# One inference step of a two-layer diffusion backbone: 48 modulation tiles move from the first attention into the first projection

## The chip, the cores and the metric

One core of a Trainium2 chip runs the whole step. The metric is the device time of one execution in microseconds, as the median of three runs, beside one execution that was profiled. TensorE multiplies matrices, VectorE and ScalarE work on tiles element by element, GpSimd issues the gathers and a few additions, SyncE issues the weight loads.

## The reference

Two trunk layers are computed for 512 latent tokens and 128 context tokens, width 1024, all in float32. Each layer does:

```
mod = SiLU(cond) @ w_mod[l] + b_mod[l]            # 6 x 1024 values; cond: c for latents, c_ctx for context
h   = RMSNorm(x) * (1 + scale1) + shift1
q, k, v = split(h @ w_in[l])                      # 1024 -> 2560, three head groups
o   = neighbourhood (A), differential (B) and grouped-query (C) attention
x   = x + gate1 * (o @ w_out[l])
h2  = RMSNorm(x) * (1 + scale2) + shift2
s   = top-16 of 128 x 128 product keys, 8 heads, of h2 @ wq
x   = x + gate2 * sum of 128 experts' v rows, weighted by gelu(u . h2) * softmax(s)
```

Context tokens read only context tokens; latents read their own keys and cached context keys. Every token has its own 128 experts, whose rows are gathered from memory (u and v, 8 KB a token and slot; 128 tokens make 1.05 MB a gather).

## The kernel before

One program holds an instruction list for each engine, and semaphores order them. The latent tokens go through the stages `norm`, `project` (20 blocks of 128 columns, `NWIN`), `attention` (80 score maps in 40 pairs: 12 pairs of group A, 16 of B, 12 of C), `out_projection` (8 blocks), `norm`, `queries` (16 blocks) and `experts` (4 x 128 slots), once a layer.

The context tokens' work is threaded through these as Python generators that each engine advances by hand. `ctx_front` is a list of steps (42 before its choice of experts): its own projection, attention, output projection and queries. The first layer's front runs in the first projection: `FRONT_P` says how many steps are advanced in each of four parts of a block, the parts standing behind the matmul pairs 1, 3, 5 and 7 (`PARTS`). Behind the 42 come 24 steps (`PICKS[0]`) in which only VectorE works: it picks the experts, one step in each part of blocks 7 to 12. `ctx_slots` then handles the context tokens' 128 expert slots: GpSimd gathers the rows (L1936), VectorE takes the dot product (L1744), ScalarE applies gelu, VectorE adds the scaled row two slots later (L1736). `ROW_CALLS` says how many slots ("calls") each engine does behind each block of the projection (P), pair of the attention (A), block of the output projection (O) and of the queries (Q). Which of nine row buffers a slot may use depends on the stages around it (`ctx_buffers`): five in the projection, six late in the attention and in the output projection, and at the seam to the queries only three.

The modulation is 48 tiles a layer (`mod_tile`: four matmuls of a 128 x 2 by 128 x 256 product over one 0.5 MB weight block), eight tiles a chunk, six chunks. ScalarE copies a finished chunk to a row (`mod_copy`, L1044), TensorE turns it (`mod_turn`, L647), VectorE adds the bias (`mod_add`, L1408). Chunks 0 and 1 of the first layer are made in the opening. `project_mods` puts chunks 2 to 5 behind blocks 0 to 3 of the first projection, eight tiles in a row. `pair_mods` puts the second layer's 48 tiles behind pairs 2 to 29 of the first attention, three, three and two in three pairs out of five; `pair_chunk` places the copy and the turn.

All weights come through one ring of four 0.5 MB buffers (`RING`). SyncE loads them in the order of `block_plan`, which repeats the order in which TensorE takes them, and waits before each until TensorE has released the buffer (L609).

In `project` TensorE waits at block i for the evacuation of block i - 2 by ScalarE, which itself has its slots of the block before ahead of it in its list. `post` adds a norm or rotation step behind blocks 4 to 15, and VectorE answers a block later. The attention starts for TensorE when all blocks are evacuated, for VectorE when it has done the projection's slots.

## Time and profile before

| | us |
|---|---|
| median of three runs | 4343.43 |
| lowest, highest | 4335.09, 4356.98 |
| the profiled execution, its own time | 4348.79 |
| its span, first to last instruction | 4346.8 |
| TensorE busy | 2888.6 (66%) |
| VectorE busy | 2806.7 (65%) |
| ScalarE busy | 1454.9 (33%) |
| GpSimd busy | 1292.9 (30%) |

The span is the time between the first and the last instruction of the profiled execution; its own time has 2.0 us more around it. Shares are means over stages that have different limits.
### The profile page before, as it was taken

The page shows a single profiled execution, that of the slowest core. Times are in us where ns is not written, and L with a number is a line of the kernel's source. Part 1 is how long each engine was busy: PE and PEld are TensorE (multiplying, and loading weights), DVE is VectorE, ACT ScalarE, POOL GpSimd, SP SyncE. Part 2 cuts the span into 40 slices and gives each one's busy share as a digit, 9 for nine tenths or more (in the row PEclk, how much of TensorE's full clock was granted, in tenths as well). Part 3 has the DMA queues.
Part 4 walks back from the last instruction along what each step waited for, and adds up shares of the span by engine and source line. Part 5 has one row for each costly group of instructions (what it writes and reads, how often), then busy time and mean ns, then how long its engine had stood idle before and what let it go on. Part 6 is the DMA issues. An engine that isn't in the chain of part 4 may idle for free.

```text
span 4346.8 us, 47495 instructions
## 1 busy us (share of the span) xinstructions
PE 2888.6 (66%) x16560; PEld 1298.9 (30%) x16560; DVE 2806.7 (65%) x5854; ACT 1454.9 (33%) x4676; POOL 1292.9 (30%) x1306
## 2 busy tenths in 40 slices
PE   7897688775666666655556978886555555555554
PEld 4456565331221122321111566543111111111111
DVE  2166887697646756665675789669764775775444
ACT  2113675332223322222223468533222222222222
POOL 1002222123333333333343222212333333333332
PEclk9898889987777778778777989997778778777777
DMA  7536997569999999999997678666999999999996
GB/s 280 204 133 259 349 378 254 206 254 404 403 407 404 403 408 407 409 412 420 418 414 310 251 253 289 224 227 249 413 420 418 412 414 418 413 416 415 416 416 283
DMA packets 229151, 1508.71 MB, mean 347 GB/s; under 512 B 25392, under 2 KB 27440, under 8 KB 63920
## 3 DMA queue, kind: packets, MB, share of 16 engines
q0 software_dynamic: 185504, 1353.53, 77.7%
q1 hardware_dynamic: 43408, 152.14, 9.5%
q8 instruction: 131, 2.15, 0.2%
q14 instruction: 108, 0.88, 0.1%
HBM read 1501.38 MB, written 4.19 MB: 346 GB/s over the span
## 4 chain that ended last, share of the span: by engine, by line
DMA 41%; PE 25%; DVE 20%; issue 6%; ACT 5%; POOL 2%; SPq 0%; DVEq 0%; ACTq 0%; POOLq 0%
DMA work<-expert_dram,work 38%; PE psum L848 10%; DVE work L1694 5%; PE psum L876 4%; DVE work L1736 4%; PE psum L695 3%; DVE work L1744 3%; PE psum L786 2%; POOL work L1954 2%; DMA ring<-w_mod_dram 2%; PE psum L699 2%; ACT work L1207 1%; PE psum L763 1%; DVE stat L1484 1%; ACT work L1198 1%
## 5 line engine op out<-in xcount | busy, mean ns | idle before, releaser
L848 PE MATMUL psum<-work 64*64 64x512 f32 x8192 | 1422.0, 825 | 1121.8 <-ACT work L1207 1087.9
L1694 DVE SCALAR_TENSOR_TENSOR work<-work,psum 128x1024 f32<-128x1024 f32 x1024 | 1247.3, 1220 | 1001.9 <-DMA work<-expert_dram,work 996.9
L1954 POOL DMA_INDIRECT work<-expert_dram,work x1024 | 983.1, 960 | 1722.9 <-PE psum L848 1586.8
L848 PEld LDWEIGHTS psum<-work 64*64 64x64 f32 x8192 | 329.6, 168 | 2157.7 <-ACT work L1207 1841.9
L1198 ACT ACTIVATE work<-work 128x2 f32<-128x2 f32 x512 | 104.1, 203 | 1926.6 <-DVE work L1694 1910.0
L1936 POOL DMA_INDIRECT work<-expert_dram,work x256 | 279.5, 1092 | 1207.6 <-DVE work L1736 888.3
L1744 DVE SCALAR_TENSOR_TENSOR work<-work 128x1024 f32<-128x1024 f32 x256 | 311.3, 1217 | 92.3 <-DMA work<-expert_dram,work 91.8
L1207 ACT ACTIVATE work<-const,work 128x128 f32<-128x128 f32 x1024 | 347.3, 386 | 0.0
L1736 DVE SCALAR_TENSOR_TENSOR work<-work 128x1024 f32<-128x1024 f32 x254 | 325.2, 1280 | 19.7 <-ACT work L1223 19.3
L800 PE MATMUL psum<-work,ring 128*128 128x512 f32 x512 | 234.9, 614 | 28.5 <-ACT work L1070 28.5
L1201 ACT ACTIVATE work<-work 128x1 f32<-128x1 f32 x1024 | 245.7, 287 | 16.8
L763 PE MATMUL psum<-work 128*128 128x128 f32 x1456 | 214.8, 308 | 39.4 <-ACT work L1132 24.0
L695 PE MATMUL psum<-work,ring 128*128 128x512 f32 x448 | 210.4, 619 | 12.2 <-ACT work L1070 12.1
L763 PEld LDWEIGHTS psum<-work 128*128 128x128 f32 x1456 | 196.3, 216 | 57.7 <-ACT work L1132 27.5
L876 PEld LDWEIGHTS psum<-work,ring 128*128 128x128 f32 x1216 | 153.1, 208 | 29.3 <-issue 26.9
L876 PE MATMUL psum<-work,ring 128*128 128x128 f32 x1216 | 157.6, 294 | 2.3 <-DMA ring<-w_in_dram 1.1
L747 PE MATMUL psum<-work 128*64 128x128 f32 x1136 | 90.5, 312 | 79.7 <-ACT work L1141 77.6
L800 PEld LDWEIGHTS psum<-work,ring 128*128 128x128 f32 x512 | 99.2, 199 | 144.4 <-issue 141.6
L1217 ACT ACTIVATE work<-work 128x1 f32<-128x1 f32 x256 | 50.3, 196 | 264.7 <-DVE work L1744 264.7
L1484 DVE TENSOR_REDUCE stat<-psum 128x1 f32<-128x640 f32 (+2 forms) x160 | 116.8, 759 | 25.9 <-PE psum L731 22.3
L1117 ACT ACTIVATE work<-psum,stat 128x640 f32<-128x640 f32 (+2 forms) x160 | 117.9, 738 | 26.2 <-DVE stat L1484 23.8
L695 PEld LDWEIGHTS psum<-work,ring 128*128 128x128 f32 x448 | 87.1, 199 | 120.6 <-issue 109.1
(197 smaller groups left out, 2864.9 us busy)
## 6 DMA issues: line engine op xcount, KB each, us to landing
ring<-w_mod_dram SPq DMA_DIRECT2D x96, 512.0 KB
ring<-w_in_dram SPq DMA_DIRECT2D x80, 512.0 KB
ring<-w_query_dram SPq DMA_DIRECT2D x64, 512.0 KB
work<-expert_dram,work POOLq DMA_INDIRECT x1280, 7.6
ring<-w_out_dram SPq DMA_DIRECT2D x32, 512.0 KB
work<-rpb_dram POOLq DMA_DIRECT2D x2, 2688.0 KB, 12.1
xT<-xT_dram SPq DMA_DIRECT2D x1, 2560.0 KB, 11.8
work<-tables_dram POOLq DMA_DIRECT2D x2, 1024.0 KB, 5.4
```

Of the source, the lines that this page charges most:

```text
L695: last = pe.matmul(out, w[:, k, :], h[:, k, :], start=(k == 0), stop=(k == KC - 1))
L763: last = pe.matmul(flat[:, at_:at_ + P], prob[:, n % NPROB, b * P:(b + 1) * P], shares_[:, n % 4, :], start=(n == first), stop=(n == end))
L800: last = pe.matmul(psum[:, s % 2, :], w[:, k, :], h[:, k, :], start=(k == 0), stop=(k == KC - 1))
L848: last = pe.matmul(out[to:to + HP, cols_], diag[tok, n % NDIAG, tok], rows[(SLOTS * t + s) % NBUF][tok, D + 512 * half:D + 512 * half + 51 ...
L876: last = pe.matmul(out, one, two, start=(k == 0), stop=(k == KC - 1))
L1201: act.activation(coef[:, s + k:s + k + 1], act_out[:, s + k:s + k + 1], ACT.Copy, scale=weight[:, t % 2, s + k:s + k + 1]).then_inc(coef_d ...
L1207: act.activation(diag[:, (n + k) % NDIAG, :], con("ident"), ACT.Copy, scale=coef[:, s + k:s + k + 1]).then_inc(diag_done, 1)
L1694: dve.scalar_tensor_tensor(u, u, 1.0, pair[0], ALU.mult, ALU.mult, accum_out=act_in[:, s:s + 1]).then_inc(dot_done, 1)
L1736: last = dve.scalar_tensor_tensor(csum, v, ccoef[:, s:s + 1], csum, ALU.mult, ALU.add)
L1744: dve.scalar_tensor_tensor(u, u, GELU_C, xrow, ALU.mult, ALU.mult, accum_out=cact_in[:, s:s + 1]).then_inc(ctx_dot, 1)
L1936: pool.indirect_dma_start(crows[b], None, a[f"expert{l}"], bass.IndirectOffsetOnAxis(cexpert[:, s:s + 1], 0)).then_inc(ctx_row_in[b], 16)
L1954: pool.indirect_dma_start(rows[m % NBUF], None, a[f"expert{l}"], bass.IndirectOffsetOnAxis(expert[:, t % 2, s:s + 1], 0)).then_inc(row_in[ ...
```

## The change

The second layer's 48 modulation tiles leave the first attention. They are taken in the first projection, blocks 7 to 18, one in each of the four parts of a block. The first layer's 32 tiles are no longer taken eight in a row but singly, between the steps of the front. `FRONT_SEQ` writes the order out: "f" a front step, "m" a tile of the first layer, "n" one of the second. In block 5 two front steps move from the first parts to the last. Chunks are copied a block after their last tile and turned two blocks after; the last of the second layer is turned at the head of the attention, which now waits for all twelve additions. The second layer's chunks use PSUM banks 6 and 7, and wait for the context work's last reads of them.

The context slots move too: the first projection takes 17 for 11 and starts them at block 13 instead of 17, the attention 68 for 76, the output projection 18 for 14, the norm behind it 2 (a new place), the queries 24 for 28. The second layer's counts stay. At its start GpSimd's first five gathers are issued ahead of the wait for the last residual and of the tables.

```diff
-FRONT_P = ([(1, 1, 1, 7), (1, 0, 0, 3), (1, 1, 1, 2), (1, 1, 1, 2), (1, 1, 1, 3), (1, 1, 1, 5), (1, 0, 0, 3)]
-           + [(1, 1, 1, 1)] * (PICKS[0] // 4) + [(0, 0, 0, 0)] * (NWIN - 7 - PICKS[0] // 4))
+FRONT_SEQ = [("fm", "fm", "fm", "mfmfmfmfmfmfmf"), ("fm", "", "", "mfmfmf"), ("fm", "fm", "fm", "mfmf"),
+             ("fm", "fm", "fm", "mfmf"), ("f", "fm", "f", "mfmfmf"), ("m", "m", "fm", "mfffffff"), ("f", "", "", "fff")]
+FRONT_SEQ += [("fn",) * 4] * (PICKS[0] // 4)
+FRONT_SEQ += [("n",) * 4] * (12 - PICKS[0] // 4)
+FRONT_SEQ += [("",) * 4] * (NWIN - len(FRONT_SEQ))
+FRONT_P = [[x.count("f") for x in parts] for parts in FRONT_SEQ]
+CHUNK_DONE = {chunk_place("m", c - 1): (0, c) for c in range(2, NCHUNK)}
+CHUNK_DONE.update({chunk_place("n", c + 1): (1, c) for c in range(NCHUNK)})
+CHUNK_COPY = {i + 1: x for i, x in CHUNK_DONE.items()}
+CHUNK_TURN = {i + 2: x for i, x in CHUNK_DONE.items()}
-ROW_CALLS = [dict(P=[0] * (NWIN - 3) + [3, 4, 4], A=shares(76, NPAIR), O=shares(14, KC), Q=shares(28, HC)),
-             dict(P=shares(28, NWIN), A=shares(60, NPAIR), O=shares(12, KC), Q=shares(29, HC))]
+ROW_CALLS = [dict(P=[0] + [0] * 13 + [2] * 4 + [3] * 3, A=shares(68, NPAIR), O=[3, 2, 2, 2, 2, 2, 2, 3] + [2],
+                  Q=shares(24, HC)),
+             dict(P=[0] + shares(28, NWIN), A=shares(60, NPAIR), O=shares(12, KC) + [0], Q=shares(29, HC))]
...
             def mod_tile(l, j):
-                if k == 0 and NCHUNK * l + c >= 2:
-                    pe.wait_ge(mod_read, NCHUNK * l + c)
+                if k == 0 and l == 0 and c >= 2:
+                    pe.wait_ge(mod_read, 3 if c == 5 else 2)
+                elif k == 0 and l:
+                    pe.wait_ge(*rd("ks", 0, 3))
+                    pe.wait_ge(*rd("ks", 0, 2))
+                    if c >= 2:
+                        pe.wait_ge(mod_read, NCHUNK * l + c - 1)
...
             def project(l, front):
-                            if l == 0 and 1 <= i < 5:
-                                mod_turn(0, 1 + i)
-                            for m, j in project_mods(l, i):
-                                mod_tile(m, j)
+                            if l == 0 and i in CHUNK_TURN:
+                                mod_turn(*CHUNK_TURN[i])
                         if l == 0 and k in PARTS:
-                            go(front, FRONT_P[i][PARTS.index(k)])
+                            for x in FRONT_SEQ[i][PARTS.index(k)]:
+                                if x == "f":
+                                    go(front, 1)
+                                else:
+                                    mod_tile(*next(mods[x]))
             def attention(l, front):
+                if l == 0:
+                    mod_turn(*CHUNK_TURN[NWIN])
+                    pe.wait_ge(mod_read, 2 * NCHUNK)
...
-                    for m, j in pair_mods(l, k):
-                        mod_tile(m, j)
-                    if pair_chunk(l, k, 4) is not None:
-                        mod_turn(l + 1, pair_chunk(l, k, 4))
...
             def norm(ni, slots):                       # VectorE
+                calls = norm_calls(ni)
+                go(slots, (calls + 1) // 2)
                 dve.wait_ge(sum_step, KC * (ni + 1))
...
         def _(pool):
                 if l:
+                    pool.wait_ge(row_used, SLOTS * LT * l)
+                    calls += ROW_CALLS[l]["P"][0]
+                    ctx_gather(l, calls)
                     pool.wait_ge(y_added, LT * l)
...
-                if l:
-                    ctx_gather(l, 0)
```

## Rows read from the trace of the kernel before

**Rows 1.** Windows: microseconds, busy time (instructions) by engine, granted clock, DMA share, GB/s.

```profile
core 0: us, PE busy (x) PEld busy (x) DVE busy (x) ACT busy (x) POOL busy (x), PEclk, DMA share, GB/s
45.00:203.00 158.00, 131.91 (x822) 79.64 (x822) 33.30 (x49) 31.06 (x63) 11.82 (x6) 0.81 0.62 215
203.00:270.00 67.00, 63.28 (x453) 53.27 (x453) 24.29 (x85) 8.86 (x15) 0.00 (x0) 1.00 0.67 233
270.00:335.00 65.00, 57.36 (x127) 24.80 (x126) 62.15 (x162) 9.18 (x15) 0.00 (x0) 0.95 0.18 58
335.00:399.40 64.40, 47.19 (x406) 45.10 (x404) 32.94 (x50) 15.68 (x50) 13.82 (x13) 0.91 0.68 251
399.40:704.60 305.20, 228.85 (x1976) 171.03 (x1976) 257.54 (x434) 217.50 (x653) 77.91 (x77) 0.87 0.90 345
798.40:971.00 172.60, 134.33 (x395) 67.54 (x395) 143.26 (x379) 55.94 (x155) 36.56 (x32) 0.89 0.64 241
971.00:2270.00 1299.00, 787.93 (x4796) 276.07 (x4796) 824.59 (x1887) 360.04 (x1280) 471.98 (x483) 0.77 1.00 408
2525.00:2765.10 240.10, 189.95 (x1540) 153.85 (x1541) 218.23 (x378) 190.40 (x566) 61.80 (x60) 0.91 0.75 264
```

**Rows 2.** Waits of TensorE from 45 to 203: total us, times, longest.

```profile
PE psum L636 <- DMA ring<-w_mod_dram: 18.4, 21, 3.9
```

**Rows 3.** Windows of the modulation tiles' line alone (L636), eight records a tile.

```profile
45.00:203.00 158.00, 26.95 (x256) 4.14 (x256) 0.81 0.62 215
399.40:704.60 305.20, 27.32 (x384) 7.56 (x384) 0.87 0.90 345
```

**Rows 4.** Timeline of TensorE: start, length, what, records, idle before and its releaser.

```profile
56.59 1.48 PE L636 MATMUL psum<-ring,cT 128*2 128x256 f32 x24
...
123.81 9.82 PE L876 MATMUL psum<-ring,work 128*128 128x128 f32 x64 [1.66 <-DMA ring<-w_in_dram]
...
228.28 14.45 PE L876 MATMUL psum<-work,ring 128*128 128x128 f32 x128
```

**Rows 5.** Timeline of VectorE: end of the picks, first and last context slot's dot.

```profile
335.62 0.23 DVE L1897 TENSOR_SCALAR work<-work 128x128 f32<-128x128 f32 x1
...
353.78 1.22 DVE L1744 SCALAR_TENSOR_TENSOR work<-work 128x1024 f32<-128x1024 f32 x1
...
396.02 1.22 DVE L1744 SCALAR_TENSOR_TENSOR work<-work 128x1024 f32<-128x1024 f32 x1 [2.91 <-DMA work<-expert_dram,work]
```

**Rows 6.** Waits of TensorE from 203 to 399.4.

```profile
PE psum L683 <- DVE work L1460: 3.4, 1, 3.4
```

**Rows 7.** Timeline of TensorE: a value block (14), the attention's first scores.

```profile
335.63 7.31 PE L699 MATMUL psum<-ring,work 128*128 128x128 f32 x64
...
382.14 0.70 PE L729 MATMUL psum<-work 64*128 64x256 f32 x4 [1.75 <-ACT work L1091]
```

**Rows 8.** DMA issues on the page: engine, count, median us from issue to landing.

```profile
work<-expert_dram,work POOLq DMA_INDIRECT x1280, 7.6
```

**Rows 9.** Groups of VectorE's instructions: first attention, then second attention.

```profile
L1736 DVE SCALAR_TENSOR_TENSOR work<-work 128x1024 f32<-128x1024 f32 x75 | 95.9, 1279 | 1.7 <-ACT work L1223 1.7
L1744 DVE SCALAR_TENSOR_TENSOR work<-work 128x1024 f32<-128x1024 f32 x75 | 91.3, 1218 | 21.0 <-DMA work<-expert_dram,work 20.6
...
L1744 DVE SCALAR_TENSOR_TENSOR work<-work 128x1024 f32<-128x1024 f32 x59 | 71.7, 1215 | 4.2 <-DMA work<-expert_dram,work 4.2
```

**Rows 10.** Timeline of VectorE: dots of context slots 100, 102 and 105.

```profile
788.90 1.22 DVE L1744 SCALAR_TENSOR_TENSOR work<-work 128x1024 f32<-128x1024 f32 x1 [5.62 <-DMA work<-expert_dram,work]
...
809.99 1.22 DVE L1744 SCALAR_TENSOR_TENSOR work<-work 128x1024 f32<-128x1024 f32 x1 [5.98 <-DMA work<-expert_dram,work]
...
836.58 1.22 DVE L1744 SCALAR_TENSOR_TENSOR work<-work 128x1024 f32<-128x1024 f32 x1 [6.42 <-DMA work<-expert_dram,work]
```

**Rows 11.** The norm products of the second layer's start (L1440): shortest, median, longest ns.

```profile
L1440 DVE TENSOR_TENSOR work<-xT,work x8: 679/2223/2226, 2363.9 to 2375.9; 128x512 f32<-128x512 f32 x8
```

More of the change, by code:

```diff
@@ L115 @@
 A_MAPS = 2 * A_PAIRS
-MOD_PAIR = 2
-MOD_CYCLE = 5
 GELU_C = math.sqrt(2.0 / math.pi)
@@ L263, in front_blocks, with mod_order @@
     return [[next(blocks) for _ in range(n)] for n in FRONT_BLOCKS] + [[]] * PICKS[l]
+def mod_order():
+    return {"m": iter([(0, j) for j in range(16, NMOD)]), "n": iter([(1, j) for j in range(NMOD)])}
 def block_plan():
@@ L269, in block_plan @@
     for l in range(L):
-        front = iter(front_blocks(l))
+        front, mods = iter(front_blocks(l)), mod_order()
         for i in range(NWIN):
             plan.append(("win", l, i))
-            for p in range(len(PARTS)):
-                if p == len(PARTS) - 1:
-                    plan += [("mod", m, j) for m, j in project_mods(l, i)]
-                if l == 0:
-                    for _ in range(FRONT_P[i][p]):
-                        plan += next(front)
-        for k in range(NPAIR + 2):
-            plan += [("mod", m, j) for m, j in pair_mods(l, k)]
+            for seq in FRONT_SEQ[i] if l == 0 else ():
+                for x in seq:
+                    plan += next(front) if x == "f" else [("mod", *next(mods[x]))]
         plan += [("wout", l, i) for i in range(KC)]
@@ L675, in post @@
                     pe.wait_ge(post_fin, POSTS * l + p - 1)
+                if l == 0 and p == 1:
+                    pe.wait_ge(mod_read, 4)
                 if what == "norm":
@@ L1052, in square, with norm @@
                 act.activation(sq[:, c % 2, :], xT[:, c, 0:NLAT], ACT.Square).then_inc(sq_ready, 1)
-            def norm(ni):
+            def norm(ni, slots):
                 if ni == 0:
@@ L1358, in _ @@
                 slots = ctx_slots(l)
-                norm(2 * l)
+                norm(2 * l, slots)
                 project(l, front, slots)
@@ L1362, in _ @@
                 out_projection(l, slots)
-                norm(2 * l + 1)
+                norm(2 * l + 1, slots)
                 queries(l, slots)
@@ L1366, in _ @@
                 experts(l, front)
-            norm(2 * L)
+            norm(2 * L, None)
         @block.vector
@@ L1414, in mod_add, with root, norm @@
                         [P, KC, 2]), ALU.add, ALU.mult))
-            def root(l, i, ps, n):
+            def root(l, i, ps, n, slots=None, calls=0):
                 dve.tensor_scalar(var, ps, 1.0 / n, EPS, ALU.mult, ALU.add).then_inc(var_ready, 1)
+                go(slots, calls)
                 dve.wait_ge(sd_ready, roots(l, i))
                 link(dve.reciprocal(rs, var))
-            def norm(ni):
+            def norm(ni, slots):
                 l, half = ni // 2, ni % 2
+                calls = norm_calls(ni)
+                go(slots, (calls + 1) // 2)
                 dve.wait_ge(sum_step, KC * (ni + 1))
@@ L1431, in norm @@
                 else:
-                    root(l, 5 if half else 0, psum[:, 2, :], D)
+                    root(l, 5 if half else 0, psum[:, 2, :], D, slots, calls // 2)
                 if ni == 2 * L:
@@ L1902, in _ @@
                 slots = ctx_slots(l)
-                norm(2 * l)
+                norm(2 * l, slots)
                 project(l, front, slots)
@@ L1906, in _ @@
                 out_projection(l, slots)
-                norm(2 * l + 1)
+                norm(2 * l + 1, slots)
                 queries(l, slots)
@@ L1910, in _ @@
                 experts(l, front)
-            norm(2 * L)
+            norm(2 * L, None)
         @block.gpsimd
@@ L1990, in _ @@
                     ctx_gather(l, calls)
+                calls += ROW_CALLS[l]["O"][KC]
+                ctx_gather(l, calls)
                 pool.wait_ge(ctx_added, SLOTS * l + last_slot(l, (3, 4, 5)) + 1)
```

48 lines of the change are left out of this document (25 added, 23 removed).

## The prediction

> **What bounds the kernel now.** I read the busy times by stage first, then who waited for whom on TensorE and VectorE, then the timelines at the seams between stages. The stage table [rows 1] shows four kinds of stretch. In the experts (971 to 2270) the DMA share is 1.00 at 408 GB/s: nothing here touches it. The first projection (45 to 399.4) is TensorE's: 131.91 of 158 us busy up to 203, 63.28 of 67 to 270; then VectorE is the one that is full, 62.15 of 65. The first attention (399.4 to 704.6, first to last softmax exponential) shows VectorE busy for 257.5 of 305.2 us and the DMA engines 0.90 busy. The second layer's attention, the same 40 pairs without modulation tiles and with 60 context-expert calls for 76, takes 240.1 with VectorE 218.2 and DMA 0.75 [rows 1]. So the DMA load is what is crowded in the first attention, and hardly used (0.18) at 270 to 335, where tiles are to go.
>
> **Term 1, blocks 0 to 6 (45 to 203): first layer's 32 tiles singly.** Now they come eight at a time behind blocks 0 to 3, and a ring of four buffers cannot feed eight in a row: TensorE waits 18.4 us for them in 21 waits [rows 2], and its 32 tiles are 26.95 us busy [rows 3], with 3.2 us more for a projection weight that stands behind a batch in the DMA queue (I take 3 from the timeline; the first such wait is 1.66, [rows 4]). Together 48 us. A tile that lies in the ring costs 1.48/3 = 0.49 us [rows 4]; 32 of them 16 us. Fed singly, each lies beside a front step of two blocks or a pair of matmuls. Supply: one tile is 0.524 MB, at 408 GB/s 1.28 us; a modulation tile and two context blocks are 3.9 us of transfer beside 0.49 + 2 x 1.8 = 4.1 us of TensorE. It just fits, with little slack in block 0, where 4.5 MB of tables and bias (11 us) land as well. Gain 48 - 16 = 32. The clock: 64 context matmul records at 123.81, behind a batch, take 9.82 us, and 128 at 228.28 take 14.45 [rows 4], that is 2.6 us more for the first; the granted clock is 0.81 here and 1.00 from 203 to 270 [rows 1]. Four such restarts are some 9 us; I take 5. Against it: a batch hid the ScalarE and VectorE latency of the context attention, whose scores, softmax and turns now follow each other closer; I charge 4. Term 1: -34 (bounds -20, if block 0 and the chain take half back, to -43).
>
> **Term 2, blocks 7 to 19 (270 to the first exponential at 399.4).** Added: 48 tiles at 0.49 = 23.5 us of TensorE, and the turns, copies and additions of six chunks, which move along and are small; 1 us of VectorE's is counted in Term 3, and TensorE's in the 3 us below. In blocks 7 to 13 VectorE is the bound: its picks run without a gap up to 335.6 [rows 5], TensorE is idle 7.6 of 65 us [rows 1] and waits for it, as 3.4 us in one place [rows 6]. 28 tiles are 13.7 us, 7.6 of it in that idle time; block 13 ends some 3 to 4 us later. If that cover is gone the tiles cost 13.7. Blocks 14 to 19 are bare TensorE work now, 7.31 us each [rows 7]; 20 tiles add 9.8, so the projection ends at 382.1 + 13 = 395 (in old times). But its end did not matter: TensorE was ready at 382.1 [rows 7] and the first exponential ran at 399.4, since VectorE and ScalarE still had slots 0 to 10 to finish, the last at 396.0 [rows 5]. With 17 slots instead of 11, and from block 13 instead of 17, the first dot moves from 353.8 to about 345 (335.6 and a gather's issue and landing, 7.6, [rows 8]), then five buffers, freed two slots late, let three slots pass in the 7.6 us of a landing and the 2.5 us of VectorE's two passes, 3.5 us a slot: slot 16 at about 395 to 398. Both chains end together; the addition of the last chunk and TensorE's new wait for it, ahead of the first scores, put 2 us behind (what is queued behind that wait is the whole attention).
> The resource that gets tight is DMA: from 335.6 on, 22 ring tiles (11.5 MB) and 17 rows of 1.05 MB (17.8 MB) are 29.4 MB, at 408 to 420 GB/s 70 to 72 us, so 406 to 408, and 2 us behind. Now: 399.4. Term 2: +10, with 6 more slots done by then. Bounds: -3 (rows need not all have landed, slots overlap) to +25.
> A rule against the change: the Trainium skill, DMA: Bandwidth & Descriptors, section Specifications, gives about 358 GB/s as the HBM limit of one core; by it the 29.4 MB would be an estimated 82 us and Term 2 +21. This trace moved 408 GB/s over 1299 us [rows 1], so the row is taken.
> New waits on TensorE: the first tile of a chunk waits for the read of its bank (6 or 7) by ScalarE or VectorE two blocks back, already done, so I charge nothing; the rest of its block is queued behind it, and a wait of a microsecond in each of six would be inside the bounds. SP issues the 48 loads in the new order, each as its buffer falls free, and so ahead of TensorE by up to four; in the attention it has then only four output blocks in the ring. GpSimd's gathers stand in their own queue.
>
> **Term 3, the first attention.** It loses 48 tiles (27.32 us of TensorE, [rows 3]; 25.2 MB, 61 us of DMA) and 8 of its calls. A call is a dot and an addition: 1.218 + 1.279 = 2.5 us of VectorE [rows 9]. VectorE's work becomes 257.5 - 8 x 2.5 - 1 = 236.5. What is left is its idle time: 47.7 us now, 20.6 of it for rows that had not landed [rows 9], against 21.9 and 4.2 in the second layer's attention [rows 1, 9]. With rows alone in the DMA queues (71 MB in 260 us, 274 GB/s) I take the second layer's idle time scaled to 68 calls, 24. 236.5 + 24 = 261 for 305.2: -44. Bounds: idle time stays 47.7, -21; it falls to 10, -58.
>
> **Term 4, output projection, norm, queries.** The output projection gets 18 calls for 14, and the norm behind it 2; the queries 24 for 28. With 2.4 us a call and 0.75 for the residual of a block against some 7.7 us of TensorE, as in the first projection (7.31 and more), two calls hide and three just do. In block 7 and the norm they don't: at the seam only three row buffers suit both stages, so each slot waits for a whole gather, 5.6 and 6.4 us at 788.9 and 836.6 [rows 10]. By the kernel's buffer rule 8 slots are so bound now, two of them ahead of the norm; after it 6, all in the queries, and two of distance four in the norm. I count about +4 ahead of the queries (the norm's first call waits some 6 us for its row, the second hides ScalarE's root) and +2 in their first four steps; behind these VectorE is full (143.3 of 172.6 for the stage, the rest mostly those waits, [rows 1]) and has 4 calls less, -10. Term 4: -4 (bounds +8, -12).
>
> **Term 5, start of the second layer.** Five gathers are issued some 8 us earlier, ahead of the tables. They landed before their use already. They may let the bias land sooner, and GpSimd's mask additions with it, beside which VectorE's eight norm products take up to 2226 ns for 679 [rows 11]. Here the Trainium skill (SBUF — State Buffer, Who interferes with whom) says that such a two-input operation and GpSimd's block each other. An earlier start could save some 4 us; but tables and bias wait for the same event as before. -1 (0 to -4).
>
> **Sum.** -34 + 10 - 44 - 4 - 1 = -73. The profiled execution took 4348.8 (span 4346.8): 4276. The median of the three runs is 4343.4, 5.4 lower, so 4271 as a time.
>
> **Rivals.** (a) The rows' latency, not the DMA load, binds the first attention: only 8 calls and a few us go, -20 for -44: 4295. For it: five or six buffers stay, and a gather takes 7.6 us to land [rows 8]. Against: 20.6 us of row waits at DMA 0.90, 4.2 at 0.75, with the same buffers. (b) Ring loads and rows halve the queues in blocks 13 to 19: 17.8 MB at 205 GB/s are 87 us, 335.6 + 87 = 423 for 408: 4286. Against: the ring has 11.5 MB to send in that time, less than half. (The Trainium skill, the same DMA page, section Queues, rings and completion order, says that each DMA engine takes its queues in turn; by that an equal split while both are full.) (c) Blocks 0 to 6 are bound by supply; half of Term 1 stays: 4288. For it: the slack of 0.2 us in 4.1 above. (d) Slower: the slots of blocks 13 to 19 stand on ScalarE ahead of the next block's evacuation, so a row that comes late holds TensorE, which then frees no ring buffer. If each of 17 slots costs a bare round trip as at the queries' seam, 8.9 us (836.6 less 810.0 is three of them, [rows 10]), they end at 345 + 151 = 496, 97 late and not 10: 4358. It makes the whole change a loss from 83 us late on, 8.1 us a slot for the 3.5 I take; five buffers for three speak against it. (e) The edit does what it says: the tiles cannot stay in the attention, so no case for that.
>
> **How the numbers follow.** Forecast 0.62 (own range 4250 to 4292); (a) 0.13; (b) 0.08; (c) 0.10; (d) 0.03, and 0.04 for a cost that I don't see; these two lie around no change. The range 4244 to 4305 holds the forecast and (a) to (c). A change under 0.5% (22 us) can't be told from none here: faster 0.93, same 0.04, slower 0.03 (the tails of (d) and of the unseen).
>
> **What would show it.** Waits of TensorE for modulation tiles up to 203 fall from 18.4 us to under 6. The first exponential comes at about 375 (399.4 - 34 + 10). The attention takes 250 to 272, DMA share near 0.7, VectorE's waits for rows under 8 us. Granted clock from 45 to 203 above 0.9. The picks end near 302. If the first exponential is later than 390, or the attention longer than 280, I am wrong in Term 2 or 3; a wait for a row in each of slots 5 to 16 would be (b) or (d).

## The result, and the profile after

| | before | after |
|---|---|---|
| median of six runs each, us | 4337.43 | 4380.80 |
| lowest, highest, us | 4328.82, 4356.98 | 4376.05, 4384.29 |
| the profiled execution's span, us | 4346.8 | 4380.4 |

The ratio is 1.0091, 95% interval 1.0076 to 1.0106: slower by 0.9%, where 4271 was forecast. The first view of the new kernel is the busy time by stretch (columns as in [rows 1]). The first two rows are the same times as there; the third begins near the start of block 7, the fourth at the end of the picks, the fifth at the first softmax exponential. The sixth is the queries, up to the first expert's dot product at 1011.3; before, that dot product came at 967.5, so the row of [rows 1] that ends at 971.0 is 3.5 us too long for this comparison.

```profile
45.00:203.00 158.00, 131.91 (x847) 85.44 (x847) 35.67 (x51) 29.45 (x59) 12.46 (x7) 0.90 0.61 221
203.00:270.00 67.00, 57.41 (x382) 45.51 (x383) 23.13 (x81) 9.16 (x17) 0.00 (x0) 0.90 0.59 199
270.00:365.40 95.40, 79.09 (x357) 29.13 (x355) 63.46 (x168) 12.33 (x24) 0.00 (x0) 0.89 0.44 162
365.40:493.50 128.10, 92.79 (x652) 65.84 (x654) 47.50 (x70) 28.50 (x91) 23.58 (x19) 0.79 0.76 292
493.50:753.40 259.90, 193.83 (x1550) 156.54 (x1546) 236.90 (x401) 199.45 (x597) 70.80 (x68) 0.91 0.77 275
848.50:1011.30 162.80, 131.53 (x392) 66.48 (x392) 130.33 (x359) 52.11 (x142) 30.37 (x28) 0.90 0.65 239
```

The attention, in the fifth row, has become 45.3 us shorter (305.2 in [rows 1], 259.9 here), as forecast. All of that and more is lost ahead of it: the first exponential comes at 493.5, not at 399.4. By stage, after less before: block 7 starts 4.4 later (274.4 for 270.0); from there to the first exponential +89.7 (219.1 for 129.4); the attention -45.3; output projection and norm +1.3; queries up to the first expert -6.3; the first layer's experts -5.9; the second layer's projection -3.6. That is +34.3 of the 33.6 between the spans.

What TensorE waited for, from 45 to 270, to 365.4, and to 493.5 (total us, times, longest; the modulation tiles' line is now L651):

```profile
PE psum L651 <- DMA ring<-w_mod_dram: 20.2, 8, 3.9
PE psum L1017 <- DVE work L1804: 6.5, 1, 6.5
...
PE psum L651 <- DMA ring<-w_mod_dram: 12.1, 5, 2.8
PE psum L713 <- DMA ring<-w_in_dram: 2.7, 5, 0.8
...
PE psum L651 <- DMA ring<-w_mod_dram: 26.2, 7, 6.5
PE psum L717 <- DMA ring<-w_in_dram: 5.2, 6, 3.2
PE psum L752 <- DVE modT L1426: 2.5, 1, 2.5
```

That is twenty waits for a tile with 58.5 us, for all 80 tiles. Before, the 32 tiles of the first layer waited 18.4 us [rows 2], and the 48 others in the attention another 15.8 (waits of TensorE, 399.4 to 704.6):

```profile
PE psum L636 <- DMA ring<-w_mod_dram: 15.8, 6, 3.7
```

So 34.2 us in 27 waits have become 58.5 in twenty. The timeline of TensorE over one block shows where they stand (start, length, what, records, idle before and its releaser):

```profile
303.09 1.03 PE L651 MATMUL psum<-ring,cT 128*2 128x256 f32 x8 [2.82 <-DMA ring<-w_mod_dram]
304.49 2.90 PE L713 MATMUL psum<-work,ring 128*128 128x512 f32 x4 [0.36 <-DMA ring<-w_in_dram]
307.32 0.61 PE L651 MATMUL psum<-ring,cT 128*2 128x256 f32 x8
307.86 1.98 PE L713 MATMUL psum<-work,ring 128*128 128x512 f32 x4
...
312.23 0.61 PE L651 MATMUL psum<-ring,cT 128*2 128x256 f32 x8
312.78 1.98 PE L713 MATMUL psum<-work,ring 128*128 128x512 f32 x4
314.60 1.02 PE L700 MATMUL psum<-work,const 128*128 128x512 f32 x2
318.17 0.61 PE L651 MATMUL psum<-ring,cT 128*2 128x256 f32 x8 [2.55 <-DMA ring<-w_mod_dram]
```

Only the last tile of a block waits, then the next block's weight behind it, and then one pair of matmuls takes 2.90 us where the others take 1.98. SyncE's own queue says why; this is its timeline over the same time:

```profile
284.58 15.19 SPq L619 DMA_DIRECT2D ring<-w_mod_dram  x4
299.82 0.43 SPq L619 DMA_DIRECT2D ring<-w_in_dram  x1
300.30 14.82 SPq L619 DMA_DIRECT2D ring<-w_mod_dram  x4
```

The ring has four buffers, and entry n lies in buffer n mod 4. A block's weight keeps its buffer until the block's last pair. The fourth entry behind that weight is the block's fourth tile (the order is weight, tile, tile, tile, tile), and it needs this very buffer. So its load is issued only when the block is over, at about 299.8, and TensorE stands until it has landed. That is a matter of the place in the ring, not of bandwidth: the DMA share in this stretch is 0.44.

The groups of TensorE's instructions from block 7 to the first exponential, before (270 to 399.4) and after (270 to 493.5), price it:

```profile
L695 PE MATMUL psum<-work,ring 128*128 128x512 f32 x112 | 50.5, 605 | 0.0
L699 PE MATMUL psum<-ring,work 128*128 128x128 f32 x384 | 43.4, 275 | 0.0
```
```profile
L713 PE MATMUL psum<-work,ring 128*128 128x512 f32 x112 | 63.1, 691 | 3.5 <-DMA ring<-w_in_dram 3.5
L717 PE MATMUL psum<-ring,work 128*128 128x128 f32 x384 | 59.0, 319 | 5.2 <-DMA ring<-w_in_dram 5.2
L651 PE MATMUL psum<-ring,cT 128*2 128x256 f32 x384 | 35.4, 447 | 38.3 <-DMA ring<-w_mod_dram 38.3
```

48 tiles are 35.4 us of TensorE (0.74 each, for the 0.49 of the forecast), 38.3 of waits for them, 8.7 of waits for weights, and the same 496 projection matmul records take 28.2 us more: 110.6 us where 23.5 were charged. 94.1 us of it show at the first exponential (493.5 for 399.4); the rest went into time in which TensorE had been idle (129.4 less 57.36 and 47.19, 24.9 us, [rows 1]).

In blocks 13 to 19 the context slots suffer from it. VectorE, from the end of the picks, waits for TensorE's turns, whose additions stand ahead of its slots (view: waits of VectorE, 365.4 to 493.5; below it, its timeline):

```profile
DVE modT L1426 <- PE psum L662: 51.0, 3, 19.0
DVE work L1765 <- DMA work<-expert_dram,work: 20.5, 5, 6.8
```
```profile
365.42 0.23 DVE L1918 TENSOR_SCALAR work<-work 128x128 f32<-128x128 f32 x1
...
374.42 1.22 DVE L1765 SCALAR_TENSOR_TENSOR work<-work 128x1024 f32<-128x1024 f32 x1 [6.84 <-DMA work<-expert_dram,work]
...
400.27 0.17 DVE L1426 TENSOR_TENSOR modT<-psum,cols 128x16 f32<-128x16 f32 x1 [18.96 <-PE psum L662]
```

The first attention's waits for rows, against 20.6 in [rows 9]:

```profile
L1765 DVE SCALAR_TENSOR_TENSOR work<-work 128x1024 f32<-128x1024 f32 x67 | 81.6, 1217 | 8.6 <-DMA work<-expert_dram,work 8.3
```

### The profile page after: what moved, and what is told of

Its sections match the earlier page's. It is cut to its first block, busy times and chain, and to the rows that moved or that the text cites. A ratio compares the mean times of both kernels' runs of the same rounds, so it can differ in the third digit from the quotient of the medians.

```text
span 4380.4 us, 47502 instructions
## 1 busy us (share of the span) xinstructions
PE 2922.1 (67%) x16560; PEld 1309.6 (30%) x16560; DVE 2803.7 (64%) x5854; ACT 1453.1 (33%) x4676; POOL 1305.4 (30%) x1306
## 4 chain that ended last, share of the span: by engine, by line
DMA 40%; PE 28%; DVE 19%; issue 6%; ACT 5%; POOL 2%; SPq 0%; DVEq 0%; ACTq 0%; POOLq 0%
DMA work<-expert_dram,work 37%; PE psum L867 10%; DVE work L1715 5%; PE psum L713 4%; DVE work L1757 4%; PE psum L895 4%; DVE work L1765 3%; PE psum L805 3%; PE psum L717 2%; POOL work L1975 2%; DMA ring<-w_in_dram 2%; ACT work L1225 1%; DVE stat L1507 1%; PE psum L786 1%; PE psum L651 1%
## 5 line engine op out<-in xcount | busy, mean ns | idle before, releaser
L819 PE MATMUL psum<-work,ring 128*128 128x512 f32 x512 | 232.1, 608 | 30.3 <-ACT work L1089 30.3
L1219 ACT ACTIVATE work<-work 128x1 f32<-128x1 f32 x1024 | 245.7, 287 | 16.8
L713 PE MATMUL psum<-work,ring 128*128 128x512 f32 x448 | 223.0, 641 | 15.0 <-ACT work L1089 9.7
L786 PE MATMUL psum<-work 128*128 128x128 f32 x1456 | 214.1, 307 | 25.5 <-ACT work L1146 10.8
## 6 DMA issues: line engine op xcount, KB each, us to landing
work<-rpb_dram POOLq DMA_DIRECT2D x2, 2688.0 KB, 15.8
xT<-xT_dram SPq DMA_DIRECT2D x1, 2560.0 KB, 11.7
```

What stands on the lines that cost most here:

```text
L713: last = pe.matmul(out, w[:, k, :], h[:, k, :], start=(k == 0), stop=(k == KC - 1))
L786: last = pe.matmul(flat[:, at_:at_ + P], prob[:, n % NPROB, b * P:(b + 1) * P], shares_[:, n % 4, :], start=(n == first), stop=(n == end))
L819: last = pe.matmul(psum[:, s % 2, :], w[:, k, :], h[:, k, :], start=(k == 0), stop=(k == KC - 1))
L1219: act.activation(coef[:, s + k:s + k + 1], act_out[:, s + k:s + k + 1], ACT.Copy, scale=weight[:, t % 2, s + k:s + k + 1]).then_inc(coef_d ...
```

## The experiments

Each was compared with the kernel before on the same chip. The three groups (e1 to e4, e5 to e7, e8 to e11) ran on different chips; across groups the ratios to before are what can be compared. The table cuts every profile at three events: the start of block 7, the first exponential, the last exponential. All but the first two rows are explained below.

| kernel | block 7 starts | to first exponential | attention | ratio to before [95%] |
|---|---|---|---|---|
| before | 270.0 | 129.4 | 305.2 | |
| after | 274.4 | 219.1 | 259.9 | 1.0091 [1.0076, 1.0106] |
| e1_m_only | 269.2 | 130.3 | 307.4 | 1.0002 [0.9987, 1.0017] |
| e2_n_only | 267.6 | 222.1 | 273.4 | 1.0135 [1.0116, 1.0153] |
| e3_rows_only | 266.5 | 132.9 | 299.8 | 0.9974 [0.9962, 0.9985] |
| e4_two_n | 269.1 | 144.1 | 287.3 | 0.9988 [0.9975, 1.0001] |
| e5_own_all | 244.6 | 187.8 | 260.3 | 0.9958 [0.9944, 0.9971] |
| e6_own_old_slots | 244.9 | 180.5 | 275.2 | 0.9993 [0.9979, 1.0006] |
| e7_two_n_new_slots | 266.7 | 141.7 | 272.0 | 0.9935 [0.9916, 0.9954] |
| e8_own_late_add | 246.0 | 192.3 | 263.5 | 0.9991 [0.9977, 1.0005] |
| e9_own_m_two_n | 242.4 | 143.9 | 274.0 | 0.9912 [0.9883, 0.9940] |
| e10_own_first_half | 245.7 | 150.0 | 281.0 | 0.9927 [0.9905, 0.9949] |
| e11_own_m2_two_n | 242.7 | 142.7 | 274.2 | 0.9879 [0.9851, 0.9906] |

**The parts one by one (e1 to e4).** e1: the first layer's tiles singly, the rest as before.

```diff
-FRONT_SEQ += [("fn",) * 4] * (PICKS[0] // 4)
-FRONT_SEQ += [("n",) * 4] * (12 - PICKS[0] // 4)
+FRONT_SEQ += [('f', 'f', 'f', 'f')] * (PICKS[0] // 4)
+FRONT_SEQ += [('', '', '', '')] * (12 - PICKS[0] // 4)
```

The second layer's 48 tiles are back in pairs 2 to 29, and `ROW_CALLS` as before.

> One part alone: the first layer's 32 tiles go singly as in the change (the front's order too), the second layer's 48 stay in the attention's pairs, slots as before. Theory R (ring order): tile or block number four behind a projection weight needs that weight's ring buffer, so its load starts only when the weight is released and TensorE waits a whole landing, 2.5 to 3 us, there. Then the stretch up to block 4's end gains some 17 us as in the changed kernel (202 to 185), blocks 5 and 6 give it back (tiles and the shifted front steps, a wait of 6 us for the context norm), and the total is within 10 us of before. Theory D (DMA bandwidth and slots in blocks 13 to 19 alone are at fault): this part keeps what I had forecast, 25 to 34 us faster than before.

4344.87 for 4343.77: no change. The waits up to block 7:

```profile
PE psum L674 <- DMA ring<-w_mod_dram: 18.4, 8, 3.4
PE psum L1045 <- DVE work L1836: 6.3, 1, 6.3
```

Spread out, the tiles wait as long in total as in batches, 18.4 us, in 8 waits for 21. Block 5 starts 12.4 us earlier than before (202.4 for 214.8), and then takes 44.6 us for 32.3: two front steps were moved to its end, and there TensorE waits 6.3 us for VectorE's norm of the context tokens (L1836), for 2.1 before.

e2: the second layer's tiles alone, with the first layer's in batches and the slots where they were.

```diff
-FRONT_SEQ = [("fm", "fm", "fm", "mfmfmfmfmfmfmf"), ("fm", "", "", "mfmfmf"), ("fm", "fm", "fm", "mfmf"),
+FRONT_SEQ = [("f", "f", "f", "mmmmmmmmfffffff"), ("f", "", "", "mmmmmmmmfff"), ("f", "f", "f", "mmmmmmmmff"),
...
```

> One part alone: the 48 second-layer tiles move into blocks 7 to 18, one per part, the first layer's stay eight in a row, slots as before (11 in the projection, from block 17). Theory R: every block from 7 to 18 takes 15 to 16 us for 7.8, with a wait of 2 to 3 us for the fourth tile and 0.3 to 0.8 for the next weight, so the first exponential comes 75 to 90 us later than 399.4, the attention is some 30 us shorter, and the total is 40 to 60 us slower than before. Theory D: blocks 7 to 12 take 10 us, blocks 13 to 18 suffer only from rows; with 11 late slots the first exponential is at most 20 us late and the total is 10 to 25 us faster.

4401.41, and the first exponential 90 us late: this part alone brings the whole loss. Its waits for tiles from 270 to 395:

```profile
PE psum L650 <- DMA ring<-w_mod_dram: 24.5, 9, 6.7
```

e3: the slots alone, with the second layer's earlier gathers (shown against the kernel before).

```diff
-ROW_CALLS = [dict(P=[0] * (NWIN - 3) + [3, 4, 4], A=shares(76, NPAIR), O=shares(14, KC), Q=shares(28, HC)),
+ROW_CALLS = [dict(P=[0] + [0] * 13 + [2] * 4 + [3] * 3, A=shares(68, NPAIR), O=[3, 2, 2, 2, 2, 2, 2, 3] + [2],
+                  Q=shares(24, HC)),
```

> One part alone: the new slot counts and places (17 in the projection from block 13, 68, 18 + 2, 24) and the second layer's earlier gathers, modulation tiles as before. Theory R: the slots are no cost; the first exponential within 5 us of 399.4, the attention 10 to 20 us shorter for 8 calls less, total 10 to 25 us faster. Theory S (slots that stand on ScalarE and VectorE ahead of the projection's evacuations hold TensorE back): first exponential 20 us or more later, total slower than before.

4334.81, 0.26% faster. The 17 slots are done when 11 were (first exponential at 399.4 in both), and the attention is only 5.4 us shorter (10 to 20 were expected), with the tiles still in it: VectorE has 18.6 us less to do (238.9 for 257.5) but is idle for 60.9 us there instead of 47.7.

e4: as e2, but two tiles a block, so that 24 of the 48 stay in the attention.

```diff
-FRONT_SEQ += [("fn",) * 4] * (PICKS[0] // 4)
-FRONT_SEQ += [("n",) * 4] * (12 - PICKS[0] // 4)
+FRONT_SEQ += [('f', 'fn', 'f', 'fn')] * (PICKS[0] // 4)
+FRONT_SEQ += [('', 'n', '', 'n')] * (12 - PICKS[0] // 4)
```

> A changed size: two second-layer tiles a block (parts 3 and 7) in blocks 7 to 18 instead of four, that is 24 tiles; the other 24 stay in the attention, in pairs 2 to 16. First layer's eight in a row, slots as before. Theory R: a ring of four then holds a weight, two tiles and the next weight, nothing stands fourth, so waits for modulation tiles in blocks 7 to 18 are under 5 us in all; first exponential at most 15 us later than 399.4, attention 10 to 20 us shorter, total 0 to 15 us faster than before. Theory T (each single tile costs TensorE several us whatever the ring does, by its weight loads or the granted clock): half of e2's loss in the projection, 35 to 45 us.

4337.63, with an interval that still touches no change. There are three entries a block now: the third behind a weight is the next block's weight, and the fourth, which needs this weight's buffer, is the next block's first tile and not one that this block needs. From 270 to 400 one wait for a tile is left, and SyncE's queue is no longer held for a block (its timeline below it):

```profile
PE psum L674 <- DMA ring<-w_mod_dram: 2.7, 1, 2.7
```
```profile
286.10 0.80 SPq L640 DMA_DIRECT2D ring<-w_mod_dram  x2
287.53 0.33 SPq L640 DMA_DIRECT2D ring<-w_in_dram  x1
```

The same order with half the tiles costs 14.7 us up to the first exponential, for 92.7 in e2. A cost of several us for every single tile, whatever the ring does, is excluded by this. But e4 halves the number of tiles along with their places in the ring, so it does not show alone how much of e2's loss is the ring; e5 does. A deeper ring for the same order (six buffers, by the same count, for five entries a block) was not tried.

**The tiles in buffers of their own (e5, e6, e8).** Two 0.5 MB buffers in idle work space, with their own semaphores, take the 32 and the 48 tiles out of the ring. The order of e5 is that of the changed kernel. One of the context slots' five row buffers had to be given up in the projection.

```diff
+def own(key):
+    return key[0] == "mod" and (key[1] == 1 or key[2] >= 16)
...
+                if own(key):
+                    n = OWN[key]
+                    if n >= 2:
+                        sp.wait_ge(own_freed[n % 2], n // 2)
...
+                    sp.dma_start(own_home(key), weights[what][l, i]).then_inc(own_landed[n % 2], 16)
-    sets = {"P": (0, 1, 2, 7, 8), "A": (0, 1, 2, 3, 8), "B": (0, 1, 2, 3, 4, 5), "O": (0, 1, 2, 3, 4, 5),
+    sets = {"P": (0, 1, 2, 7, 8) if l else (0, 1, 2, 8), "A": (0, 1, 2, 3, 8), "B": (0, 1, 2, 3, 4, 5), "O": (0, 1, 2, 3, 4, 5),
```

> The suspected cause alone taken away: the changed kernel, order of TensorE's work and slots as they are, but the 80 modulation tiles of both layers that are taken in the projection get two buffers of their own (space idle at that time; the first layer's context slots give up one of five row buffers in the projection for it). The ring of four then holds only projection and context weights. Theory R: waits for modulation tiles fall from 20 + 33 us to under 8, the picks end at 300 to 315 for 365, first exponential at 370 to 395 for 493, and the total is 4265 to 4300, 40 us or more faster than before: my forecast's terms hold once the ring is out of the way. Theory T (single tiles cost more than their records; clock, weight loads) or a share of VectorE waiting for TensorE's turns: picks still after 340, total within 15 us of before or slower.

4326.70: 1.3% faster than the changed kernel by the two ratios, but far from the forecast; the picks end at 319 and the first exponential comes at 432.4, so neither theory fits whole. Its waits, up to 270 and then to 432:

```profile
PE psum L1048 <- DVE work L1835: 9.0, 1, 9.0
PE psum L682 <- DMA work<-w_mod_dram: 4.0, 3, 1.8
...
PE psum L682 <- DMA work<-w_mod_dram: 12.7, 5, 4.3
PE psum L783 <- DVE modT L1457: 10.7, 1, 10.7
```

Block 5 starts at 179.1, 35.7 us ahead of before, which is Term 1's gain; block 5 itself then gives back 11 (43.3 us for 32.3). From block 7 to block 13 a block takes 11.6 us, for 15.5 in the changed kernel and 9.3 before. But from block 13 to the first exponential it is 118.4 us, for 73.7 before. VectorE waits there for rows and for the turns, while the DMA share is 0.85:

```profile
DVE work L1796 <- DMA work<-expert_dram,work: 35.0, 10, 5.8
DVE modT L1457 <- PE psum L693: 28.6, 3, 11.8
```

From block 7 to the first exponential the ring out of the way is worth 31.3 us (187.8 for 219.1), 23.6 of them ahead of block 13. That is a third of the 89.7; 58.4 are left. The two new buffers are a ring too, of two entries, and SyncE now waits for them and hardly for the ring of four (waits of SyncE's queue, 270 to 432.4):

```profile
SPq L642 <- PE psum L682: 110.9, 38, 7.6
SPq L647 <- PE psum L748: 13.2, 2, 10.0
```

e6 is e5 with the slots at their old counts and places (`ROW_CALLS` of before): are the early slots at fault?

> As e5, but with the slots before (11 in the projection from block 17, 76, 14, 28; gathers in their old place). It tells what the slots add once nothing stalls. Theory R with my Terms: the first exponential is as early or some us earlier than e5's, the attention 15 to 25 us longer, total 5 to 20 us slower than e5. If the earlier slots hold the projection (VectorE waits for turns of chunks ahead of its slots in every second block), e6 is as fast as e5 or faster.

4336.76, slower than e5. From block 13 to the first exponential it still takes 113.8 us, with 11 slots for 17, and so the slots are not what makes it long. Here TensorE is through block 19 at 398.6 and then waits for the last chunk's addition, which stands on VectorE behind the slots: the wait that I had priced at 2 us.

```profile
PE psum L782 <- DVE modT L1456: 17.1, 1, 17.1
```

Block 13 alone takes 19.0 us. SyncE's queue (first) and TensorE (second) show how long it is from issue to use once gathers are under way:

```profile
318.88 0.43 SPq L646 DMA_DIRECT2D ring<-w_in_dram  x1
320.97 17.62 SPq L641 DMA_DIRECT2D work<-w_mod_dram  x4
```
```profile
326.71 0.61 PE L681 MATMUL psum<-work,cT 128*2 128x256 f32 x8 [3.04 <-DMA work<-w_mod_dram]
330.56 3.76 PE L747 MATMUL psum<-ring,work 128*128 128x128 f32 x16 [3.23 <-DMA ring<-w_in_dram]
```

The weight that was issued at 318.88 could first be used at 330.56, 11.7 us later, and the four tiles behind it held SyncE's one list for 17.6 us: they have buffers of their own, but stand in the same list of loads, and the weight had waited in that list behind the tiles of block 13.

e8 is e5 with the additions behind the slots of a block on VectorE, not ahead.

```diff
-                    if l == 0 and i in CHUNK_TURN:
+                    if l == 0 and i in CHUNK_TURN and CHUNK_TURN[i][0] == 0:
                         mod_add(*CHUNK_TURN[i])
...
                     go(slots, ROW_CALLS[l]["P"][i + 1])
+                    if l == 0 and i in CHUNK_TURN and CHUNK_TURN[i][0]:
+                        mod_add(*CHUNK_TURN[i])
```

> e5 (own buffers for all 80 tiles) with one order changed on VectorE: the addition of a second-layer chunk, which waits for TensorE's turn at a block's end, stands behind the block's context slots and not ahead of them. Theory V (in e5 the slots from block 13 on are held by these waits, 12 + 10 + 7 us in three blocks): from the picks' end (319) to the first exponential 85 to 100 us for 113, total 10 to 25 us faster than e5's 4327. Theory L (row landings and the ring's loads share the DMA engines, so a slot takes 5 to 6 us whatever stands ahead of it): under 8 us faster than e5.

4332.15, not faster than e5. VectorE waits 23.2 us for turns, 28.4 for rows and 10.9 for ScalarE, together as long as e5's 63.6: the order on VectorE was not what held the stretch.

**Fewer tiles where they are dear (e7, e9, e10, e11).** e7 is e4 with the new `ROW_CALLS`, all in the ring.

> e4's placing (two second-layer tiles a block, 24 in all, the rest in the attention) with e3's slots. If the two gains add: 6 + 9 us, some 15 us faster than before, 4325 to 4332. If they collide (17 slots from block 13 on behind VectorE's wait for turns), it is no faster than e3 alone, 4335.

4311.57. That is 29 us, nearly twice the sum of e3 and e4 (9 and 6): with 24 tiles gone from the attention, its 8 fewer calls count, 272.0 us for 287.3 in e4, where with all 48 in it they brought 5.4 (e3).

e9 is e7 with two changes to the first layer's 32 tiles: they go singly, in the order of the changed kernel, and have e5's separate buffers, at a time when the row buffers are still idle, so that all five can stay. The second layer's 24 stay in the ring. e1 has shown that the order alone brings nothing. The edit of `own` against e5:

```diff
 def own(key):
-    return key[0] == "mod" and (key[1] == 1 or key[2] >= 16)
+    return key[0] == "mod" and key[1] == 0 and key[2] >= 16
```

> Own buffers for the first layer's 32 single tiles only; second layer's as in e7 (two a block in the common ring, 24 of 48, the rest in the attention), slots as the change has them. Theory R: blocks 0 to 4 as in e5, block 5 starts at about 179 for 210, block 5 keeps its wait of 9 us for the context norm, so blocks 7 on come 20 us earlier than in e7 and stay so: total 4290 to 4297, e7's 4311 less 15 to 20. Rival: the stretch behind the picks absorbs it (rows bind), under 8 us faster than e7.

4296.99, 0.2% under e7 by the ratios, whose intervals overlap. Block 7 starts at 242.4 for 266.7 in e7, 24.3 us earlier; 20.1 of it are left at the last exponential (660.3 for 680.4). The two profiled spans are only 6.5 us apart (4297.9 for 4304.4), since e9's profile is longer in the experts, whose code is the same: 1376.0 for 1367.8 from the first to the last dot product of the first layer's.

e10 moves the same 24 tiles, but four a block into blocks 7 to 12, with buffers of their own and none from block 13 on.

```diff
-FRONT_SEQ += [('f', 'fn', 'f', 'fn')] * (PICKS[0] // 4)
-FRONT_SEQ += [('', 'n', '', 'n')] * (12 - PICKS[0] // 4)
+FRONT_SEQ += [('fn', 'fn', 'fn', 'fn')] * (PICKS[0] // 4)
+FRONT_SEQ += [('', '', '', '')] * (12 - PICKS[0] // 4)
```

> e5 cut to the tiles that lie under VectorE's picks: four second-layer tiles a block in blocks 7 to 12 (24), own buffers, the other 24 in the attention; slots as the change has them. Term 2's claim is that these are hidden: picks end as in e5, 317 to 321, and blocks 14 to 19 run at 7.2 to 8 us each; first exponential at 385 to 400 for e5's 432, attention 10 to 15 us longer than e5's 260, total 4300 to 4312. If instead TensorE's added work in blocks 7 to 12 is what delays the picks, they end no earlier than e7's less 20, 312, and the total is above 4315.

4306.43. With no tiles behind block 13, 17 slots and four row buffers, block 13 to the first exponential takes 84.2 us, for 118.4 in e5. So 34.2 us of what e5 lost there was the doing of the tiles behind block 13. The attention, with 24 tiles in it, is 281.0 us, 20.7 longer than e5's where 10 to 15 were expected, and longer than e9's 274.0; why was not looked into.

e11 is e9 with the wait in block 5 taken away: the two front steps go back, and the tiles behind them move to earlier blocks.

```diff
-FRONT_SEQ = [("fm", "fm", "fm", "mfmfmfmfmfmfmf"), ("fm", "", "", "mfmfmf"), ("fm", "fm", "fm", "mfmf"),
-             ("fm", "fm", "fm", "mfmf"), ("f", "fm", "f", "mfmfmf"), ("m", "m", "fm", "mfffffff"), ("f", "", "", "fff")]
+FRONT_SEQ = [("fm", "fm", "fm", "mfmfmfmfmfmfmf"), ("fm", "", "m", "mfmfmfm"), ("fmm", "fmm", "fm", "mfmfm"),
+             ("fm", "fm", "fm", "mfmf"), ("fm", "fm", "fm", "fff"), ("f", "f", "f", "fffff"), ("f", "", "", "fff")]
```

> e9 with the first layer's tiles put earlier (10, 6, 8, 5, 3 in blocks 0 to 4, none in block 5) and the front's steps of block 5 as before the change (1, 1, 1, 5), since chunk 4, which the context's second norm needs, is then turned a block earlier. Theory N (the shifted steps of block 5 leave VectorE's norm bare behind the block, 9 us): block 5 takes 30 to 34 us for 43, TensorE's wait for the norm is under 3 us, total 5 to 12 us faster than e9, the fastest version. Rival: block 5 gains but the picks, bound by VectorE, end as in e9; no faster than e9.

4284.94, 0.9879 [0.9851, 0.9906]: the fastest, 1.2% under the kernel before and, by the two ratios, 2.1% under the changed one. The wait for the norm falls from 9.0 (e9, first row) to 2.1 (e11, second row; both up to 308):

```profile
PE psum L1077 <- DVE work L1868: 9.0, 1, 9.0
```
```profile
PE psum L1077 <- DVE work L1868: 2.1, 1, 2.1
```

But what the wait gave back was spent elsewhere. Block 5 is 33.6 us long for 44.1 and starts 10.8 later (186.9 for 176.1), since the tiles put into earlier blocks make these longer (block 2 takes 23.9 us for 16.2), and block 7 starts where it did. So the 12 us over e9 do not come from the edit's place: 8 of them lie in the first layer's experts (1367.6 us for 1376.0), whose length varied between 1365 and 1376 in these profiles with the same code. Why e11 is the faster one is not explained here, and part of it may be no property of the edit.

## Why the prediction was wrong

**Term 2, blocks 7 to 19: the step that failed.** Forecast +10, measured +89.7. TensorE's wait for the tiles was priced at nothing. The sentence "A tile that lies in the ring costs 0.49 us" was applied to 48 tiles of which one in four cannot lie in the ring, and "SP issues the 48 loads in the new order, each as its buffer falls free, and so ahead of TensorE by up to four" is where I should have counted positions. With four entries between two weights, a ring of four makes the last tile wait for the end of its own block. I reckoned supply in MB per us and never wrote down which entry shares a buffer with which. e2 shows the whole loss by this part alone, and e4 shows the waits gone with three entries a block. By e5 the place in the ring of four is a third of the 89.7, 31.3 us; the rest comes from four tiles a block that do not fit behind the picks (13.7 in e5, blocks 7 to 12) and from blocks 13 to 19 (44.7, of which e10 shows 34.2 to be the tiles' doing). The picks, forecast to end near 302, ended at 365.4.

The cost of it has two sizes. In blocks 7 to 12 the changed kernel takes 15.5 us a block, 11.6 with separate buffers (e5; 11.0 to 11.4 in e6, e8 and e10), 9.3 with two tiles in the ring (e7), and 9.3 before. So two tiles a block were really hidden behind the picks, as argued; four were not, even without the ring's fault: 1.7 to 2.3 us more a block. 4 x 0.55 is more than the 1.1 us a block that TensorE had been idle (7.6 us in seven blocks, [rows 1]).

From block 13 on the forecast had the slots at 3.5 us each and the DMA engines full for 70 to 72 us with 29.4 MB. Two terms were missing. The blocks' own weights and those of the output projection belong to the sum: in e5 35.4 MB moved from 319 to 432.4, which at 408 GB/s is 87 us. And the queues were not full (share 0.85, and 0.76 in the changed kernel): loads and gathers took long to land (11.7 us for a weight in e6), each wait held the engine that frees the next buffer, and with four tiles a block there was one such wait in nearly every block. e10 shows that the tiles bring this about, e6 that the slots alone do not, e8 that VectorE's order is not it. How much is landing time and how much the order of SyncE's single list was not separated, so for these blocks the cause is shown only as far as: the tiles do it, not the slots. The wait for the last chunk's addition, priced at 2 us together with that addition, was 2.5 in the changed kernel, but 10.7 in e5, 15.2 in e4 and 17.1 in e6: it was cheap only where TensorE came late anyway. In e9 and e11, with 12 tiles there and five row buffers, the share is 0.95 and 17 slots take 77 to 78 us, 4.6 each.

**Term 1: -34 forecast, none measured by block 7 (+4.4; e1 -0.8).** The reason that I gave for the gain, that a tile fed singly finds itself in the ring, fails for the same cause: waits for tiles are 17.8 us by 203 in the changed kernel, where under 6 was forecast. Rival (c) had named supply, but by bandwidth. That the gain is there when the ring is out of it, e5 shows: -35.7 at the start of block 5. The block 5 edit, which the working left at nothing, makes that block 11 to 12 us longer in e1, e5 and e9: 4 to 7 of it are the longer wait for VectorE's norm, which the steps moved to the block's end had been covering, and 2 are its four tiles. e11 takes that back and block 7 still starts no earlier, so what sets its start once the ring is out of it was not found. The granted clock rose about as forecast, 0.81 to 0.90, and brought nothing that these waits did not take, with 1.00 to 0.90 in the next stretch [rows 1].

**Term 3: right.** Attention 259.9, forecast 261; VectorE 236.9, forecast 236.5; DMA share 0.77, forecast near 0.7; waits for rows 8.3, forecast under 8, just missed. The second layer's attention was a good measure for a stage with the tiles gone. The half step too: with 24 tiles left in it and 68 calls e7, e9 and e11 take 272 to 274, though e10 takes 281. Rival (a) falls: with the tiles gone and all 76 calls still there (e2) the attention is 273.4, 31.8 shorter, and VectorE's idle time falls from 47.7 to 18.3; with the calls gone and the tiles there (e3) it is 5.4 shorter.

**Term 4: right in sum.** +1.3 and -6.3, for +4 and -8. **Term 5**: -3.6 at the second layer's projection, at the far end of 0 to -4. The runs bear this out: the projection takes 155.6 to 155.8 us in all eight kernels with the earlier gathers and 159.4 in the five without, before, e1, e2, e4 and e6. **Not forecast**: the experts of the first layer, the same code, -5.9, inside the 11 us by which they vary.

**The rivals.** (b) supposed full queues; the share was 0.76, and only five slots of 17 waited for a row (20.5 us), not each of 5 to 16. (d) had the right sign, size and place: "97 late" for 94 measured. Its mechanism, the bare round trip of each slot, is not what happened: e2 is as late with the slots where they were. (d) did say that a held TensorE frees no ring buffer; the ring held it first. Its chance of 0.03 was that of a mechanism that I had in view; that of a loss in Term 2 as a whole, whose two chains I had ending together with nothing to spare, deserved far more.

## What to carry to other kernels

In a ring of R buffers filled in order, write down for each entry which one lies R places before it, and when that one is released: behind an entry that is held for a whole block (a stationary weight), the R-th must not be one that the same block needs, nor one that is needed as soon as the block ends. Four tiles behind it in a ring of four cost a full landing a block, with the DMA engines busy for 0.44 of the time. By the same count three tiles would put the next block's weight in that place; that was not run. Buffers apart from the ring help as far as they are enough: two for four tiles a block, filled from the same list, became the next thing to wait for. And where work moves into a gap, the gap's idle time (here 1.1 us a block) is what it can take; more is paid on that engine, and again by whatever shares its list of loads.

## What the runs showed of the hardware

A wait for a 0.5 MB load that was issued only at the last moment was 2.8 us at most while the DMA share was 0.44 (five waits, 12.1 us), and up to 6.5 us at 0.76 with gathers in flight; from issue to use it was 11.7 us in e6.

A single modulation tile took 0.55 us of TensorE's progress at its best, for 0.49 in a batch. Its records are 0.61 us at a granted clock of 1.00 (2.4 GHz) and 1.03 at 0.50 (1.2 GHz). The pair of matmuls behind the wait of 2.82 us at 303.09 took 2.90 us, for 1.98 later in the block (windows of the changed kernel, columns as in [rows 1]):

```profile
303.00:306.00 3.00, 2.55 (x10) 0.94 (x11) 1.24 (x4) 0.00 (x0) 0.00 (x0) 0.50 0.97 380
308.00:312.00 4.00, 4.00 (x16) 1.32 (x16) 0.00 (x0) 0.00 (x0) 0.00 (x0) 1.00 0.02 6
```

Not every such wait is followed by the lower clock: behind one of 2.53 us at 310.69 in e2 the pair took 1.96. The granted clock was 0.89 in the stretch with the short waits and 0.79 where they were longest (365.4 to 493.5), each a mix of the two levels; that makes an estimated 75 us at the lower one, for 18 before (0.95 and 0.91, [rows 1]). The 28.2 us that 496 unchanged records took longer stand beside 12 waits for tiles; the sum had priced a wait by its own length alone. By the Trainium skill, TensorE: Matmul & The Clock Gate, section What's actually happening, 1.2 GHz is the default state and activity releases the full clock; the trace agrees, in that 0.50 stands behind a wait of 2.82 us, and 1.00 is back while the matmuls run.
